# Expert stage of a two-layer decoder trunk: float32 products with the weights stationary and 96 token slots streaming

## What is computed

```python
def _moe_swiglu(h, w_router, w_gate, w_up, w_down):
    logits = (h @ w_router).astype(jnp.float32)
    top_val, top_idx = lax.top_k(logits, TOP_K)
    top_w = jax.nn.softmax(top_val, axis=-1)
    combine = jnp.sum(jax.nn.one_hot(top_idx, N_EXPERTS, dtype=jnp.float32) * top_w[..., None], axis=-2)
    ...
    for e in range(N_EXPERTS):
        out = out + combine[..., e:e + 1] * _swiglu(h, w_gate[e], w_up[e], w_down[e])
```

## Time and profile before

| what | value |
|---|---|
| median of three executions | 1530.99 us (1530.94 to 2025.26) |
| span of the profiled execution | 1530.3 us |
| expert stage within it, first to last product | 534.1 to 1517.6 us |
| loaded weights | 430.75 MB in all, 352 MB of them in the expert stage |

### The profile page before, as it was taken

One profiled execution on the slowest core, in us unless ns is written; L12 is line 12 of the kernel. 1 busy time (PEld: TensorE's weight loads), 2 busy tenths in 40 slices (PEclk: granted clock), 3 DMA queues, 4 the chain that ended last, 5 costly groups with the idle time before them and its releaser, 6 DMA issues.

```text
span 1530.3 us, 20635 instructions
## 1 busy us (share of the span) xinstructions
PE 1485.2 (97%) x7842; PEld 1268.3 (83%) x7842; DVE 1154.3 (75%) x872; ACT 1007.7 (66%) x834; POOL 15.5 (1%) x44
## 2 busy tenths in 40 slices
PE   5999999999999799999999999999999999999997
PEld 5898899997898688888888888888888888888775
DVE  4356644445456689888888888989889988888996
ACT  4568543344568477767767767777777777776775
POOL 3000000000000000000000000000000000000000
PEclk9999999999999899999999999999999999999998
DMA  9433455554433389999999989999999998998993
GB/s 342 139 115 109 165 180 179 178 192 154 149 125 111 124 305 372 370 326 376 377 319 373 373 323 373 375 336 355 373 370 326 375 374 317 375 376 320 351 368 119
DMA packets 185376, 430.75 MB, mean 281 GB/s; under 512 B 9048, under 2 KB 11096, under 8 KB 185328
## 3 DMA queue, kind: packets, MB, share of 16 engines
q1 hardware_dynamic: 181920, 426.27, 77.7%
q0 software_dynamic: 1184, 3.22, 0.7%
q10 hardware_dynamic: 2224, 0.59, 0.2%
HBM read 429.01 MB, written 1.05 MB: 281 GB/s over the span
## 4 chain that ended last, share of the span: by engine, by line
PE 89%; ACT 4%; DVE 3%; issue 2%; DMA 1%; ACTq 0%; DVEq 0%
PE ps L1264 81%; PE ps L1605 2%; PE ps L1635 2%; DMA wif<-in_w_in_dram 1%; ACT whi L454 1%; DVE wlo L835 1%; ACT L464 1%; PE ps L1411 1%; PE ps L1283 1%; DVE y L857 0%; PE ps L1672 0%; PE ps L1670 0%; PE ps L1424 0%; DVE y L1022 0%; ACT qkc L626 0%
## 5 line engine op out<-in xcount | busy, mean ns | idle before, releaser
L835 DVE TENSOR_TENSOR wlo<-raw,whi 128x2048 fp32r<-128x2048 f32 x405 | 926.4, 2291 | 294.3 <-ACT whi L454 293.9
L454 ACT ACTIVATE whi<-raw 128x2048 fp32r<-128x2048 f32 x405 | 776.8, 1919 | 409.2 <-PE ps L1264 408.3
L1264 PE MATMUL ps<-whi,xT_hi 128*128 128x512 f32 x1056 | 418.7, 397 | 1.5 <-DVE wlo L835 1.5
L1264 PE MATMUL ps<-wlo,xT_hi 128*128 128x512 f32 x1056 | 412.6, 391 | 0.0
L1264 PE MATMUL ps<-whi,xT_lo 128*128 128x512 f32 x1056 | 411.7, 390 | 0.0
L1264 PEld LDWEIGHTS ps<-wlo,xT_hi 128*128 128x128 f32 x1056 | 198.4, 188 | 42.5
L1264 PEld LDWEIGHTS ps<-whi,xT_hi 128*128 128x128 f32 x1056 | 198.9, 188 | 41.1 <-issue 1.7
L1264 PEld LDWEIGHTS ps<-whi,xT_lo 128*128 128x128 f32 x1056 | 199.1, 188 | 39.3
L1264 PE MATMUL ps<-whi,hid_hi 128*128 128x512 f32 (+1 forms) x536 | 210.9, 393 | 0.7 <-DVE hid_lo L1150 0.7
L1264 PE MATMUL ps<-wlo,hid_hi 128*128 128x512 f32 (+1 forms) x536 | 208.7, 389 | 0.0
L1264 PE MATMUL ps<-whi,hid_lo 128*128 128x512 f32 (+1 forms) x536 | 208.7, 389 | 0.0
(11 more groups left out here) (218 smaller groups left out, 854.9 us busy)
## 6 DMA issues: line engine op xcount, KB each, us to landing
raw<-in_moe_w_gate_dram SPq DMA_DIRECT2D x112, 1024.0 KB, 5.1
raw<-in_moe_w_up_dram SPq DMA_DIRECT2D x112, 1024.0 KB, 5.3
raw<-in_moe_w_down_dram SPq DMA_DIRECT2D x112, 1024.0 KB, 5.1
raw<-in_w_in_dram SPq DMA_DIRECT2D x28, 1024.0 KB, 5.2
raw<-in_ffn_w_gate_dram SPq DMA_DIRECT2D x10, 1024.0 KB, 5.2
raw<-in_ffn_w_up_dram SPq DMA_DIRECT2D x10, 1024.0 KB, 5.1
raw<-in_ffn_w_down_dram SPq DMA_DIRECT2D x10, 1024.0 KB, 4.9
raw<-in_w_out_dram SPq DMA_DIRECT2D x8, 1024.0 KB, 4.9
```

What stands on the lines that cost most here:

```text
L454: act.activation(whi[:, i % NSPLIT, :], raw[:, i % NRAW, :], ACT.Copy).then_inc(hi_ready, 1)
L835: dve.tensor_tensor(wlo[:, i % NSPLIT, :], raw[:, i % NRAW, :], whi[:, i % NSPLIT, :].bitcast(F32), ALU.subtract).then_inc(lo_ready, 1)
L1264: ins = pe.matmul(acc, lhs, rhs, start=start and m == 0, stop=stop and m == 2, skip_group_check=True)
```

## The change

Only the expert stage is rewritten.

- **Stationary and streaming operands swap, and the splits go.** `columns` takes 128x128 blocks of the landed weights in `raw` as the stationary operand and streams 96 gathered token slots (`CAP = 96`, `xg`) as plain float32. A piece of gate or up takes 16 such matmuls, a piece of down (`down_job`) too; so a job has 42 x 16 = 672 float32 matmuls. No piece of the experts is split on ScalarE or VectorE.
- **Hidden values come out with hidden columns on the partitions**, so `hid_transpose` and the hidden split go. ScalarE's SiLU and VectorE's product are 384 numbers wide instead of 512.
- **The result comes out transposed**: ScalarE copies it (`out_columns`, 768 wide), TensorE transposes it in 8 parts (`out_rows`), ScalarE and VectorE split it (1024 wide on 96 partitions, once a job instead of two halves), then `scatter` as before, one half of the tokens at a time.
- **Buffers**: seven for gate and up, two for down, the last three in space that the mixers used for `qsT`, `ksT`, `qkc`, `vs`, `om`. SyncE orders down pieces separately, waiting on `down_used`.
- **Overflow**: an expert with more than 96 tokens gets an extra job (up to two per expert, five in all).
- The first three expert pieces are no longer split ahead of the router.

```diff
 PIECE = 2048
 
+CAP = 96
+NPIPE = 7
+NDOWN = 2
...
 MOE_BASE = 2 * MIX_PIECES + FFN_PIECES
-EXTRA = 3
+LEVELS = 2
+EXTRA = 5
...
-        raw = sb("raw", [P, NRAW, PIECE])
+        raw = sb("raw", [P, NPIPE + NDOWN, PIECE])
...
+        silu_e = scratch[:, 0:384].rearrange("p (c n) -> p c n", c=4)
+        hid_e = scratch[:, 384:1152].rearrange("p (f c n) -> p f c n", f=2, c=4)
...
+        xg = scratch[:, 1152:1920].rearrange("p (k n) -> p k n", k=KC)
...
+                def columns(f, w, o):
+                    for half in range(2):
+                        s = 4 * f + o + half
...
+                        else:
+                            sp.wait_ge(piece_used, loop.at("piece", MOE_BASE + s - NPIPE + 1))
+                        sp.dma_start(raw[:, s % NPIPE, :].rearrange("p (k n) -> p k n", k=4),
+                                     w[half * 512:(half + 1) * 512, f * FB:(f + 1) * FB].rearrange(
+                                         "(k p) n -> p k n", p=P)).then_inc(gate_in[s % NPIPE], 16)
+
...
+                def rows_down(f):
+                    for half in range(2):
+                        d = 2 * f + half
...
+                            sp.wait_ge(down_used, loop.at("down", d - NDOWN + 1))
+                        r0 = f * FB + 256 * half
+                        sp.dma_start(raw[:, NPIPE + half, :].rearrange("p (k n) -> p k n", k=2),
+                                     down[r0:r0 + 256, :].rearrange("(k p) n -> p k n", p=P)
+                                     ).then_inc(down_in[half], 16)
...
                 for f in range(EB):
...
+                    columns(f, gate, 0)
+                    if f >= 2:
+                        rows_down(f - 2)
+                    columns(f, up, 2)
+                rows_down(EB - 2)
+                rows_down(EB - 1)
...
+            def e_silu(b):
+
+                act.wait_ge(piece_used, loop.at("piece", n + 4 * b + 2))
+                if b:
+                    act.wait_ge(e_hid, loop.at("block", b))
+                act.activation(silu_e[:].rearrange("p c n -> p (c n)"),
+                               ps[:, (b % EB) % 2, 0:4 * CAP], ACT.Silu).then_inc(e_sil, 1)
+
+            def out_columns():
+
+                act.wait_ge(down_used, loop.at("down", JOB_DOWNS))
+                act.activation(outT[:].rearrange("p (b d) n -> p b (d n)", b=2),
+                               ps[:, 6:8, 0:4 * CAP], ACT.Copy).then_inc(outT_ready, 1)
+
...
+            def hidden_job(b):
+
+                dve.wait_ge(piece_used, loop.at("piece", n + 4 * b + 4))
+                dve.wait_ge(e_sil, loop.at("block", b + 1))
+                if b % EB >= 2:
+                    dve.wait_ge(down_used, loop.at("down", 2 * (b - 1)))
+                dve.tensor_tensor(hid_e[:, (b % EB) % 2].rearrange("p c n -> p (c n)"),
+                                  ps[:, 2 + (b % EB) % 2, 0:4 * CAP],
+                                  silu_e[:].rearrange("p c n -> p (c n)"), ALU.mult
                                   ).then_inc(e_hid, 1)
...
+            def out_rows():
+
+                dve.wait_ge(o_hi_ready, loop.at("job", 1))
+                dve.tensor_tensor(o_lo[:], ps[0:CAP, 4:6, :], o_hi[:].bitcast(F32), ALU.subtract
+                                  ).then_inc(o_ready, 1)
...
-            def product(i, bank, gathering=None):
...
+            def columns(s, m, gathering=None, first=False):
+
+                b = s // 4
+                bank = 2 * m + (b % EB) % 2
+                if b >= 2:
+                    pe.wait_ge((e_sil, e_hid)[m], loop.at("block", b - 1))
...
-                    hi, lo = piece(n + i + half, 4)
-                    for k in range(4):
-                        kk = 4 * half + k
-                        ins = passes(ps[:, bank, :], xT_hi[:, kk, 0:P], xT_lo[:, kk, 0:P],
-                                     hi[:, k, :], lo[:, k, :], start=half == 0 and k == 0,
-                                     stop=half == 1 and k == 3, weights_move=True)
...
+                    w = raw[:, i % NPIPE, :].rearrange("p (k n) -> p k n", k=4)
+                    for c in range(4):
+                        for k in range(4):
+                            ins = pe.matmul(ps[:, bank, CAP * c:CAP * c + CAP],
+                                            w[:, k, c * P:(c + 1) * P], xg[:, 4 * half + k, :],
+                                            start=half == 0 and k == 0 and c == 0,
...
             def down_job(f):
                 pe.wait_ge(e_hid, loop.at("block", f + 1))
-                down_piece_job(f, 0)
-                if f == EB - 2:
-                    hid_transpose(EB - 1)
-                down_piece_job(f, 1)
-
-            def scatter():
-
+                if f == 0:
+                    pe.wait_ge(tile0_done, loop.at("job", 1))
+                for half in range(2):
+                    pe.wait_ge(down_in[half], loop.at("down_in", 16 * (f + 1)))
+                    w = raw[:, NPIPE + half, :].rearrange("p (k n) -> p k n", k=2)
+                    for kk in range(2):
+                        for d in range(KC):
+                            ins = pe.matmul(ps[:, 6 + d // 4, CAP * (d % 4):CAP * (d % 4) + CAP],
+                                            w[:, kk, d * P:(d + 1) * P],
+                                            hid_e[:, f % 2, 2 * half + kk, :],
+                                            start=(f, half, kk, d % 4) == (0, 0, 0, 0),
+                                            stop=(f, half, kk) == (EB - 1, 1, 1),
+                                            skip_group_check=True)
+                    ins.then_inc(down_used, 1)
+
+            def out_rows():
+
+                pe.wait_ge(outT_ready, loop.at("job", 1))
+                for d in range(KC):
+                    ins = pe.transpose(ps[0:CAP, 4 + d // 4, (d % 4) * P:(d % 4) * P + P],
+                                       outT[:, d, :], ident[:])
+                ins.then_inc(o_ps, 1)
+
...
             def rest_of_job(then_next):
-                for f in range(1, EB):
-                    if f == 1:
-                        pe.wait_ge(job_done, loop.at("job", 1))
-                        pe.wait_ge(scatT_ready, loop.at("job", 1))
-                    else:
-                        pe.wait_ge(e_prod, loop.at("block", f - 1))
-                    product(gate_piece(f, 0), 2 * (f % 2))
-                    hid_transpose(f - 1)
-                    product(gate_piece(f, 0) + 2, 2 * (f % 2) + 1)
+                down_job(0)
+                for f in range(2, EB):
+                    columns(4 * f, 0)
+                    columns(4 * f + 2, 1)
                     down_job(f - 1)
-                if then_next:
+                if not then_next:
+                    down_job(EB - 1)
+                    out_rows()
+                    pe.wait_ge(scatT_ready, loop.at("job", 1))
+                    scatter(0)
+                    scatter(1)
+                else:
                     gather(1)
-                down_job(EB - 1)
-                if then_next:
-                    product(JOB_PIECES, 0, gathering=1)
-                scatter()
-                if then_next:
-                    scatter_matrix()
-                    product(JOB_PIECES + 2, 1)
+                    down_job(EB - 1)
+                    columns(JOB_SPLITS, 0, gathering=1)
+                    out_rows()
+                    columns(JOB_SPLITS + 2, 1)
+                    scatter(0)
+                    columns(JOB_SPLITS + 4, 0)
+                    scatter(1)
+                    columns(JOB_SPLITS + 6, 1)
+                    scatter_matrix(1)
```

More of the change, by code:

```diff
@@ L267, in trunk @@
         X_MIX, X_FFN, X_ROUTE = (0, 6), 4, 10
-        PER_JOB = {"piece": JOB_PIECES, "block": EB, "job": 1, "tile": TT, "half": 2}
+        PER_JOB = {"piece": JOB_SPLITS, "down": JOB_DOWNS, "block": EB, "job": 1, "tile": TT,
+                   "half": 2, "gate_in": 16 * JOB_SPLITS // NPIPE, "down_in": 16 * JOB_DOWNS // NDOWN}
         @block.sync
@@ L351, in _ @@
-            with sp.Fori(0, E) as j:
-                loop.reg, loop.per = j, {"piece": JOB_PIECES}
+                gate, up, down = expert(moe_w_gate), expert(moe_w_up), expert(moe_w_down)
+                def columns(f, w, o):
+                    for half in range(2):
+                        s = 4 * f + o + half
+                        if first and s < NRAW:
+                            sp.wait_ge(lo_ready, MOE_BASE - NRAW + (s - MOE_BASE) % NRAW + 1)
+                        elif first and s < NPIPE:
+                            sp.wait_ge(z_ps, 4 * DEPTH)
+                        else:
[3 more added lines that the diff above has]
+                                         "(k p) n -> p k n", p=P)).then_inc(gate_in[s % NPIPE], 16)
@@ L353, in _ @@
+                for f in range(EB):
+                    columns(f, gate, 0)
[4 more added lines that the diff above has]
+                rows_down(EB - 1)
+            loop.per = PER_JOB
+            job(0, first=True)
```

(25 more changed lines are left out.)

329 lines of the change are left out of this document (129 added, 200 removed).

## The result

The changed kernel takes 1869.37 us (four runs, 1867.78 to 1871.53) against 1531.68 for the kernel before in the same comparison: a ratio of 1.2215, interval 1.2196 to 1.2235. One of the four executions of before was slow, 2025.26 us; it is in that median and not in the ratio. Slower was forecast, at 1816.5 us; the measurement is 52.9 us above that and 5 us above the top of the range.

What follows compares the result with a forecast made beforehand. TensorE was taken to bound the expert stage, transfers close behind. 534.1 ahead + 1200.0 products + 25.0 gathers + 7.9 transposes + 12.7 scatter + 5 kind changes + 14.7 waits + 16.5 tail, with 0.65 outside, gave 1816.5 us; range 1793 to 1864.

Steps and rivals of the forecast that it cites:

- What bounds the kernel: Expert stage: TensorE sets the pace at 122.9 us a job; transfers are close behind at 116.8.
- the 0 put for it: Expert stage: dropping 42 splits a job on each of ScalarE and VectorE gains 0, as they were behind TensorE.
- The 3% that TensorE could win at most: Expert stage: taking work off TensorE wins at most 6 us a job, 49 in all, before transfers bound it.
- The price of one of the new matmuls: Expert products: two instructions at 111.6 ns, 224 ns a matmul, paced by weight loads; 150.0 us a job.
- The scatter wait: Before the scatter: TensorE waits 2.1 us for VectorE's low part of the result, seven times, 14.7 us.
- Kind changes: On TensorE: changes between the two kinds of matmul, about eight a job at some 0.1, 5 us in all.
- The tail: From the last down product to the end: 12.7 us becomes about 16.5.
- the fourth rival: At each job's start: loads come late, 35 us more, 1851 us; chance 0.08, shared with other waits of that size.
- the third: Expert stage: an expert with over 96 tokens costs an extra job, 1983 us; chance 0.03.
- The step that failed: Sum for the expert stage: lists TensorE's work per job, with no term for the loop's jump back.
- The first rival: Expert stage: the clock falls to 0.50, 2950 us, or 1927 if down for a tenth; chance 0.04.
- The second rival: Expert products: streaming sets the pace at 81 ns an instruction, loads hide, transfers decide; 1491 us; chance 0.03.

Runs made afterwards that it cites:

- experiment 10: Changed kernel with VectorE making the scatter's tiles before the next hidden product, loop kept, half of the expert matmuls left out; 1485.93 us, ratio 0.9708.
- experiment 3: Changed kernel with TensorE's loop over jobs written out and VectorE's scatter tiles made before the next job's hidden product; 1804.4 us, ratio 1.1798.
- experiment 4: Changed kernel with 128 slots instead of 96, loops and order as in the change; 1869.36 us, ratio 1.2202.
- experiment 6: Kernel of experiment 3 with 72 and with 60 of the 96 slots streamed in the expert products; 1808.91 us and 1811.7 us.
- experiment 7: Kernel of experiment 3 with 64 of 128 weight columns loaded for each expert matmul, 96 slots streaming; 1530.58 us, ratio 1.0005.
- experiment 2: Changed kernel with VectorE making the scatter's tiles ahead of the next job's hidden product; 1845.38 us, ratio 1.2054.
- experiment 1: Changed kernel with TensorE's loop over jobs written out as seven copies, the other engines' loops kept; 1830.62 us, ratio 1.1959.
- experiment 8: Kernel before with two jobs in the body of TensorE's loop, three turns and one job written out; 1537.62 us, ratio 1.0040.
- experiment 11: Kernel of experiment 2 with one in four gate and up matmuls and every second down matmul left out, 1,931 instructions between jumps; 1509.56 us.
- experiment 12: Kernel of experiment 2 with one in four gate and up and one in four down matmuls left out, 2,155 instructions between jumps; 1586.0 us.

## Why the prediction was right in direction and too low

- **What bounds the kernel** was read rightly: TensorE, with the transfers close behind. Nothing in the time is left that taking the splits off ScalarE and VectorE could have gained, which agrees with the 0 put for it; no run takes them off alone. The 3% that TensorE could win at most is what experiment 10 shows with half of the matmuls gone.
- **The price of one of the new matmuls** was right: 111.6 ns an instruction forecast, 111.6 measured in experiment 3. Experiments 4, 6 and 7 show why: the 128-column load sets it, at 60, 72, 96 and 128 columns streaming alike. 1200 of the 1816 us rested on it.
- **The scatter wait** was right in place and size: 2.1 us each as forecast, released by L1177. Its price was not: the term counted the wait alone, and experiment 2 showed 3.0 to 3.4 us for each, since a stretch at clock 0.50 follows six of the seven.
- **Kind changes**, forecast at 5 us, come to about 1 if every other term is right: the stage of experiment 3 is 2.3 us below a sum that has them, with one piece late by 1.6 us in it. **The tail** came to 17.3 for 16.5. **SyncE** kept up; one piece in 336 was late, so the fourth rival (35 us of late loads) is false, as is the third: 112 gate loads, no extra job.
- **The step that failed** is the sum's silence on TensorE's loop. It took the body over as if a turn cost nothing, which before it did (208 ns, hidden). The change takes the body from 1,210 to 2,827 instructions, most of which the forecast itself counts (1,344 instructions with a load each, a job), and six turns then cost 26.9 us. Experiments 1, 8, 10, 11 and 12 show this cause. Beside it the sum has no term for the clock behind a wait, 25.1 us. Either of the two alone would have left the time within the range; both together put it 5 us above.
- **The first rival** asked for the clock in the wrong place. It weighed whether 81 of 112 ns of streaming keep it up, over the whole stage, and gave 0.04. With 96 columns the clock held: experiment 3 runs at 1.00 through the whole stage. The half clock came behind waits of 2.1 and 4.5 us instead, the first of which the forecast had itself predicted. The earlier trace rows had the sign of it, the first gather at 0.50 after a wait; the forecast used that row for the price and not for what follows a wait.
- **The second rival**, streaming sets the pace, is false with 128 weight columns; its 81 ns is what experiment 7 measured with 64.

Not settled: where between 1,483 and 1,931 instructions the step lies; why 48 columns lose the clock and 60 keep it; why some short waits are followed by a stretch at half clock and others not (the first scatter wait of each run, the two of 2.4 us in experiment 8 and those of up to 1.6 us in experiment 7 were not). The plain float32 product with the tokens as the stationary side was not tried.

## What to carry to other kernels

Count weight loads, not columns: a plain float32 matmul is two instructions with a load each, and with 128 weight columns each costs 112 ns with 8 columns streaming as with 128, as long as the clock holds (it did not with 48 through a whole stage). Three passes of 512 columns (0.227 us each) beat it here because each load there hides behind its stream. And when a change makes a loop's body longer, look at the branch's own duration in the sequencer's rows and at the instruction queue's traffic; where the body no longer stays, write the loop out, which cost nothing here. Look at the granted clock behind a short wait on TensorE as well: here 2.1 us of waiting cost 3.0 to 3.4.

## What the runs showed of the hardware that was not expected

- A compare-and-branch that jumps back takes TensorE's sequencer 0.2 us with 1,210 and 1,483 instructions in the loop's body, and 5.6 to 6.3 us with 1,931 to 2,827, with nothing between. In the trace of the changed kernel and those of experiments 2, 8, 11 and 12 a packet of the instruction queue falls into each of the long ones.
- With 48 columns streaming behind each 128-column load, and no idle time, the granted clock was 0.50 through nearly all of the stage (2887 us); with 60 it was 1.00 until the stage's last 10 us (1812 us).
- Behind six of seven waits of 2.1 us 3.4 us ran at 0.50, and 6.8 behind each of 4.4 to 4.8 us (10.2 behind the first one of experiment 2).
- Transfers reached 395 GB/s in slices of experiment 10, where the best slice before was 377.
